# Key normalisation through a logarithm and an exponential on ScalarE, and two small TensorE products moved later, in a two-block hybrid model on one core

## The chip, the core and the metric

One Trainium2 chip, one of its cores. The metric is the device time of one execution in microseconds (us); lower is better. TensorE runs the products, VectorE (DVE in the rows), ScalarE (ACT) and GpSimd (POOL) run the elementwise work, SyncE (SP) issues the loads.

## The reference, cut to what matters

The kernel computes two transformer blocks, one after the other, for 512 tokens of width 1024: a gated-delta-rule block and then a block with stick-breaking attention and an RWKV-7 time mix, each with its feed-forward layers, all in f32. The change lies in the second block, between the projection by `w_in` and the scans. There every channel group of the RWKV part needs its key normalised per head, its decays and its bonus:

```python
p = p + (p_prev - p) * mu
w = -jax.nn.softplus(-(w0 + jnp.tanh(xw) @ w_up)) - 0.5
decay = jnp.exp(-jnp.exp(w.astype(jnp.float32)))
a = jax.nn.sigmoid(a0 + xa @ a_up)
kk = (k * k_k).astype(jnp.float32).reshape(B, L, H, N)
kk = kk / jnp.maximum(jnp.sqrt(jnp.sum(kk * kk, axis=-1, keepdims=True)), 1e-12)
k = k * (1.0 + (a - 1.0) * k_a)
...
bonus = jnp.sum(rh * kh * r_k.astype(jnp.float32), axis=-1, keepdims=True) * vh
```

## The kernel before

Every large product takes f32 operands as two parts, upper and lower (`HH`, `HL` for the activations, `WH`, `WL` for the weights), and sums three products of parts. A slab is 128x1024 numbers of weights (512 KB). SyncE loads it into one of four buffers `RAWS`; ScalarE copies its upper part into one of three buffers `WH` (line 1622, called through `begin`, always two slabs ahead); GpSimd subtracts it to get `WL` (line 2090); TensorE runs it in eight blocks of six matmuls (line 489, `slab_gemm`).

The stage of the change projects four groups, i = 0 to 3, of 128 channels. A group has six slabs. Three are of the RWKV part, for r, k and v, which VectorE takes out of PSUM and mixes with the token before (`shifted`, lines 1392, 1394, 1396, into `R1`, `K1`, `VB`). Three are of the attention, for q, k and v (`attention_inputs`, lines 1411 and 1413, 1417, 1422), after which TensorE transposes the attention's v (line 846) and ScalarE copies the transposes out (lines 1958, 1960).

Beside the three attention slabs run the `features` of the group. TensorE: the low-rank products (line 820), the sum of squares of the key over a head (line 826, into banks 4 and 5 of PSUM), the bonus product (line 834, bank 6). VectorE: `cs` (1431), `kk` (1433), `dcs` (1436), `max` (1438), `rec` (1440), `kn` (1443), `f1` (1446), `wc` (1447), `f2` (1451), `bm` (1453), `f3` (1457), `tm` (1459), `kf` (1461), `f4` (1464), `bo` (1466), `bn` (1473). ScalarE: two sigmoids (1926, 1931), `sq` (1936), the square root (1939), two exponentials (1942, 1944) and a third (1947).

Each engine's queue is written by generators: `alternate(features(i), ai, ai, ai)` takes one step of `features` and then three steps of `attention_inputs`, in turn, on each engine by itself. On TensorE a step of the latter is one block of a slab, so a `yield` more in `features` puts what follows it three blocks later. Nothing but semaphores ties the engines together, and each executes its queue in order: an instruction that waits holds all behind it. The waits that matter:

- line 826 waits for `sq` on ScalarE, and this for `kk` on VectorE;
- line 834 waits for `bo` on VectorE, the end of the chain of features;
- line 846 waits for the attention's v in SBUF (line 1422), which stands behind the features in VectorE's queue;
- the first slab product of a bank pair waits until VectorE has emptied it two slabs earlier (`shifted_bank`);
- after the last group, the heads and the scan of the next stage (from line 938 and line 865 on) wait for a memset on GpSimd (line 2195), and this for `bn` of group 3.

`EX` is one scratch tile. It holds the squares, then the clamped sums, the root, its reciprocal, and then the exponentials, so these steps follow one another. Two functions of ScalarE that are not in one table need a load of the other table between them.

Of the kernel before, what the change touches and what calls it, by code (L numbers as in the profile page):

```python
# [100 lines left out]
def alternate(*streams):  # L101

    live = list(streams)
    while live:
        for s in list(live):
            if next(s, alternate) is alternate:
                live.remove(s)


def finish(stream):  # L110
    for _ in stream:
        pass
# [34 lines left out]
def program(nc, xT, metaT, cols, consts, slabs, lup, gup, out):  # L147
    f32, f32r = mybir.dt.float32, mybir.dt.float32r
    ALU, ACT = mybir.AluOpType, mybir.ActivationFunctionType
# [6 lines left out]
    def steps(name, *names):  # L156
        return Steps(sem(name), *names)
# [205 lines left out]
    sh = steps("sh", "diff", "mix")  # L363
    lx = steps("lx", "tanh", "copy", "sigm")
    fp = steps("fp", "w", "a", "sq", "bon")
    fa = steps("fa", "sw", "sa", "sq", "rt", "e1", "e1p", "e2")
    fd = steps("fd", "cs", "kk", "dcs", "max", "rec", "kn", "f1", "wc", "f2", "bm", "f3", "tm", "kf", "f4", "bo", "bn")
    at_ev = steps("at_ev", "q0", "q1", "k", "v")
    at_vt = steps("at_vt", "t0", "t1")
    at_tr = count("at_tr")  # L370
# [106 lines left out]
    def tensor():  # L477
# [328 lines left out]
        def projected(which, j, job, ready=None):  # L806
            return slab_gemm(which, j, shifted_bank(job), HH, HL, KT, H2, ready)
# [4 lines left out]
        def features(i):  # L812
            te.wait_ge(s_k2, 64)
            if i:
                te.wait_ge(*fd.at("max", i - 1))
                te.wait_ge(*fd.at("bn", i - 1))
            te.wait_ge(*lx.at("copy"))
            for nm, r0, pr_ in (("w", 0, 2), ("a", 32, 3)):
                for q in range(2):
                    ins = te.matmul(pair(pr_)[:, q, :], LUP[r0:r0 + 32, 128 * i:128 * i + 128],  # L820
                                    LX[r0:r0 + 32, 264 * q:264 * q + 264], start=True, stop=True)
                ins.then_inc(*fp.up(nm, i))
            yield
            te.wait_ge(*fa.at("sq", i))
            for q in range(2):
                ins = te.matmul(PS[:, 4 + q, 0:288], con("bones"), EX[:, 288 * q:288 * q + 288], start=True, stop=True)
            ins.then_inc(*fp.up("sq", i))
            yield
            yield
            yield  # L830
            yield
            yield
            te.wait_ge(*fd.at("bo", i))
            te.matmul(bank(6), con("bones"), K1[:, 64:TP], start=True, stop=True).then_inc(*fp.up("bon", i))
            yield

        def attention_inputs(i):
            for s in range(3):
                yield from projected("w_in2", 12 + 4 * s + i, 2 + 7 * i + 3 + s)
            yield  # L840
            te.wait_ge(*at_ev.at("v", i))
            ps = shifted_bank(2 + 7 * i + 6)
            b = 2 * ((2 + 7 * i + 6) % 2)
            for j in range(5):
                o = PS[:, b, 128 * j:128 * j + 128] if j < 4 else PS[:, b + 1, 0:128]
                ins = te.transpose(o, VS[:, 128 * j:128 * j + 128], con("ident"))
            ins.then_inc(*at_tr.up(i))

        for i in range(4):
            for s in range(3):  # L850
                finish(projected("w_in2", 3 * i + s, 2 + 7 * i + s))
            ai = attention_inputs(i)
            alternate(features(i), ai, ai, ai)


        def rw_prepare(n):
# [155 lines left out]
    def vector():  # L1012
# [411 lines left out]
        def features(i):  # L1424
            yield
            ve.wait_ge(*fa.at("sw", i))
            ve.wait_ge(s_k2, 64)
            if i:
                ve.wait_ge(*fa.at("e2", i - 1))
                ve.wait_ge(*fd.at("f3", i - 1))  # L1430
            ve.tensor_tensor_scan(CS, RES[:, :], SW, 0.0, ALU.mult, ALU.add).then_inc(*fd.up("cs", i))
            ve.wait_ge(*sh.at("mix", 2 + 3 * i + 1))
            ve.tensor_scalar(KK, K1, col("kk", i), None, ALU.mult).then_inc(*fd.up("kk", i))
            yield
            ve.wait_ge(*fd.at("cs", i))
            ve.tensor_tensor(SW, CS, SW, ALU.subtract).then_inc(*fd.up("dcs", i))
            ve.wait_ge(*fp.at("sq", i))
            ve.tensor_scalar(two(EX), PS[:, 4:6, 0:288], 1e-24, None, ALU.max).then_inc(*fd.up("max", i))
            ve.wait_ge(*fa.at("rt", i))
            ve.reciprocal(EX, EX).then_inc(*fd.up("rec", i))  # L1440
            yield
            ve.wait_ge(*fd.at("rec", i))
            ve.tensor_tensor(KK, KK, EX, ALU.mult).then_inc(*fd.up("kn", i))
            ve.wait_ge(*fa.at("e1", i))
            ve.wait_ge(*sh.at("mix", 2 + 3 * i))
            ve.tensor_tensor(AR[:, i, :, 1, :], ch(R1), ch(EX), ALU.mult).then_inc(*fd.up("f1", i))
            ve.tensor_copy(WCC[:, i, :], ch(EX)[:, :, 63]).then_inc(*fd.up("wc", i))
            yield
            ve.wait_ge(*fa.at("e1p", i))
            ve.wait_ge(*fd.at("kn", i))  # L1450
            ve.scalar_tensor_tensor(AR[:, i, :, 0, :], ch(KK), -1.0, ch(SW), ALU.mult, ALU.mult).then_inc(*fd.up("f2", i))
            ve.wait_ge(*fd.at("f2", i))
            ve.tensor_tensor(KK, KK, SA, ALU.mult).then_inc(*fd.up("bm", i))
            yield
            ve.wait_ge(*fd.at("bm", i))
            ve.wait_ge(*fa.at("e2", i))
            ve.tensor_tensor(BK[:, i, :, 0, :], ch(KK), ch(EX), ALU.mult).then_inc(*fd.up("f3", i))
            ve.wait_ge(*f_kam.at(0))
            ve.tensor_scalar(SA, SA, col("ka", i), KAM[:, i:i + 1], ALU.mult, ALU.add).then_inc(*fd.up("tm", i))
            ve.wait_ge(*fd.at("tm", i))  # L1460
            ve.tensor_tensor(K1, K1, SA, ALU.mult).then_inc(*fd.up("kf", i))
            yield
            ve.wait_ge(*fd.at("kf", i))
            ve.tensor_tensor(BK[:, i, :, 1, :], ch(K1), ch(EX), ALU.mult).then_inc(*fd.up("f4", i))
            ve.wait_ge(*fd.at("f4", i))
            ve.scalar_tensor_tensor(K1[:, 64:TP], R1[:, 64:TP], col("rk", i), K1[:, 64:TP], ALU.mult,
                                    ALU.mult).then_inc(*fd.up("bo", i))
            yield
            ve.wait_ge(*fp.at("bon", i))
            ve.wait_ge(*sh.at("mix", 2 + 3 * i + 2))  # L1470
            if i == 3:
                ve.wait_ge(s_bs[0], 16)
            ve.tensor_tensor(TMP[i % 3][:, 0:512], VB[:, i, 128:64 + TP], bank(6), ALU.mult).then_inc(*fd.up("bn", i))

        for i in range(4):
            if i:
                ve.wait_ge(*fd.at("bn", i - 1))
            else:
                ve.wait_ge(*lx.at("sigm"))
            for s, dst in enumerate((R1, K1, VB[:, i, 64:64 + TP])):  # L1480
                shifted("w_in2", 3 * i + s, 2 + 3 * i + s, 2 + 7 * i + s, dst, 4 * s + i, 128)
            ai = attention_inputs(i)
            alternate(features(i), ai, ai, ai)


        def rw_prepare(n):
# [124 lines left out]
    def scalar():  # L1611
# [309 lines left out]
        def features(i):  # L1921
            ae.wait_ge(*fp.at("w", i))
            ae.wait_ge(*fz.at("sw"))
            if i:
                ae.wait_ge(*fd.at("f2", i - 1))
            ae.activation(two(SW[:, PAD:TP]), pair(2), ACT.Sigmoid, bias=col("w0", i)).then_inc(*fa.up("sw", i))
            ae.wait_ge(*fp.at("a", i))
            ae.wait_ge(*fz.at("sa"))
            if i:
                ae.wait_ge(*fd.at("kf", i - 1))  # L1930
            ae.activation(two(SA[:, PAD:TP]), pair(3), ACT.Sigmoid, bias=col("a0", i)).then_inc(*fa.up("sa", i))
            yield
            ae.wait_ge(*fd.at("kk", i))
            if i:
                ae.wait_ge(*fd.at("f4", i - 1))
            ae.activation(EX, KK, ACT.Square).then_inc(*fa.up("sq", i))
            yield
            ae.wait_ge(*fd.at("max", i))
            ae.activation(EX, EX, ACT.Sqrt).then_inc(*fa.up("rt", i))
            yield  # L1940
            ae.wait_ge(*fd.at("kn", i))
            ae.activation(EX, CS, ACT.Exp, scale=-KAPPA).then_inc(*fa.up("e1", i))
            ae.wait_ge(*fd.at("dcs", i))
            ae.activation(SW, SW, ACT.Exp, scale=-KAPPA).then_inc(*fa.up("e1p", i))
            yield
            ae.wait_ge(*fd.at("wc", i))
            ae.activation(EX, CS, ACT.Exp, scale=KAPPA).then_inc(*fa.up("e2", i))
            yield
# [509 lines left out]
```

## Time and profile before

| what | value |
|---|---|
| three runs | 2178.99, 2170.0 and 2177.69 us, median 2177.69 |
| the profiled execution's own time | 2169.75 us |
| its span | 2168.5 us |
| mean granted clock of TensorE | 0.966 |
| busy | PE 92%, PE weight load 77%, DVE 37%, POOL 35%, ACT 33% |
| the stage of the four groups | about 1216 to 1418 us from the start |

The profiled execution lies 0.25 us below the fastest of the three runs and 7.94 us below their median. A busy share is one of the whole span; what the change does is decided in the stage, whose own rows stand further below.

### The profile page before, as it was taken

Reading aid. Unit: us, or ns where it says so; the run is one execution under the profiler, and the core shown is the slowest. Engines: PE = TensorE matmul, PEld = TensorE weight load, DVE = VectorE, ACT = ScalarE, POOL = GpSimd, SP = SyncE. Lnnn points to the kernel's source line nnn. Section 1 sums busy time; section 2 is a strip of 40 time slices with the busy share of each in tenths; the row PEclk is TensorE's granted clock in tenths of the full one; section 3 lists DMA queues with packets and bytes.
Section 4 is the critical chain, followed back from the end, with each engine's and each line's share of the span. In section 5 each row is a group of like instructions: output and inputs, shape, how many; then the busy total and the mean of one; then the engine's idle time right before and its main releaser. Section 6 shows DMA issues by size and latency. Waiting matters only on the chain. (4 is left out here: it accounts for less than half of the span.)

```text
span 2168.5 us, 32158 instructions
## 1 busy us (share of the span) xinstructions
PE 1991.5 (92%) x13960; PEld 1674.6 (77%) x13960; DVE 794.9 (37%) x1065; ACT 705.6 (33%) x1056; POOL 763.2 (35%) x444
## 2 busy tenths in 40 slices
PE   3889988999999999999999888888999789999997
PEld 2657767777888889999999877866666568888885
DVE  6664453232111013443310466643443433434201
ACT  2453221333222333222222333254554333222222
POOL 2322120434444554444444332211111144444453
PEclk9999999999999999999999999998998899999999
DMA  7332220324332232232222422100000322332331
GB/s 272 115 119 98 79 79 32 116 78 145 117 97 90 90 102 88 88 94 91 84 88 93 131 59 63 30 6 2 2 2 2 126 69 89 96 97 89 98 91 62
DMA packets 55723, 182.76 MB, mean 84 GB/s; under 512 B 7552, under 2 KB 7808, under 8 KB 55456
## 3 DMA queue, kind: packets, MB, share of 16 engines
q1 hardware_dynamic: 55584, 180.72, 25.4%
q8 instruction: 110, 1.80, 0.3%
q14 instruction: 29, 0.24, 0.0%
HBM read 175.45 MB, written 5.24 MB: 83 GB/s over the span
## 5 line engine op out<-in xcount | busy, mean ns | idle before, releaser
L2090 POOL TENSOR_TENSOR WL<-RAWS,WH 128x1024 fp32r<-128x1024 f32 (+2 forms) x275 | 649.0, 2363 | 983.4 <-ACT WH L1622 983.4
L489 PE MATMUL PS<-HH,WH 128*128 128x264 f32 (+2 forms) x2184 | 673.1, 350 | 48.4 <-issue 12.9
L489 PE MATMUL PS<-HL,WH 128*128 128x264 f32 (+2 forms) x2184 | 657.4, 343 | 0.0
L489 PE MATMUL PS<-HH,WL 128*128 128x264 f32 (+2 forms) x2184 | 654.3, 341 | 0.0
L489 PEld LDWEIGHTS PS<-HH,WH 128*128 128x128 f32 (+1 forms) x2184 | 380.7, 192 | 117.4 <-issue 36.6
L1622 ACT ACTIVATE WH<-RAWS 128x1024 fp32r<-128x1024 f32 (+2 forms) x275 | 283.9, 1033 | 455.1 <-PE PS L489 402.1
L489 PEld LDWEIGHTS PS<-HH,WL 128*128 128x128 f32 (+1 forms) x2184 | 380.5, 191 | 48.4 <-issue 0.4
L489 PEld LDWEIGHTS PS<-HL,WH 128*128 128x128 f32 (+1 forms) x2184 | 380.9, 191 | 47.1 <-issue 1.6
L489 PE MATMUL PS<-IHf,WH 128*128 128x512 f32 (+1 forms) x704 | 209.4, 338 | 0.0
L489 PE MATMUL PS<-IHf,WL 128*128 128x512 f32 (+1 forms) x704 | 209.2, 338 | 0.0
L489 PE MATMUL PS<-ILf,WH 128*128 128x512 f32 (+1 forms) x704 | 209.2, 338 | 0.0
L1369 DVE TENSOR_TENSOR TMP<-TMP,PS 128x512 f32<-128x512 f32 (+1 forms) x66 | 45.8, 693 | 251.0 <-PE PS L489 244.0
L1889 ACT ACTIVATE IHf<-TMP 128x512 fp32r<-128x512 f32 (+1 forms) x66 | 42.0, 636 | 283.2 <-DVE TMP L1369 283.2
L489 PEld LDWEIGHTS PS<-ILf,WH 128*128 128x128 f32 x704 | 120.6, 188 | 14.9
L489 PEld LDWEIGHTS PS<-IHf,WH 128*128 128x128 f32 x704 | 120.5, 188 | 14.8
L489 PEld LDWEIGHTS PS<-IHf,WL 128*128 128x128 f32 x704 | 120.4, 188 | 14.9
L1364 DVE TENSOR_TENSOR TMP<-TMP,RSTD 128x528 f32<-128x528 f32 (+1 forms) x44 | 104.5, 2375 | 41.1 <-ACT TMP L1885 41.1
L1376 DVE SCALAR_TENSOR_TENSOR X<-PS,X 128x528 f32<-128x528 f32 (+1 forms) x16 | 11.2, 700 | 222.5 <-PE PS L489 222.5
L1357 DVE TENSOR_TENSOR TMP<-PS,RSTD 128x528 f32<-128x528 f32 (+1 forms) x44 | 30.8, 700 | 150.9 <-PE PS L489 150.2
L2106 POOL TENSOR_TENSOR SQA<-SQA,TMP 128x512 f32<-128x512 f32 (+1 forms) x39 | 54.9, 1408 | 80.4 <-ACT TMP L1635 79.7
L1371 DVE TENSOR_TENSOR ILf<-TMP,IHf 128x512 fp32r<-128x512 f32 (+1 forms) x66 | 48.7, 737 | 46.4 <-ACT IHf L1889 46.4
L1635 ACT ACTIVATE TMP<-X 128x512 f32<-128x512 f32 (+1 forms) x42 | 26.1, 627 | 86.7 <-DVE X L1376 35.7
(493 smaller groups left out, 1917.0 us busy)
## 6 DMA issues: line engine op xcount, KB each, us to landing
RAWS<-w_w_in SPq DMA_DIRECT2D x52, 512.0 KB, 4.3
RAWS<-w_ada SPq DMA_DIRECT2D x32, 512.0 KB, 3.6
RAWS<-w_f0g SPq DMA_DIRECT2D x22, 512.0 KB, 3.6
RAWS<-w_f0u SPq DMA_DIRECT2D x22, 512.0 KB, 3.5
RAWS<-w_f1g SPq DMA_DIRECT2D x22, 512.0 KB, 3.6
RAWS<-w_f1u SPq DMA_DIRECT2D x22, 512.0 KB, 3.6
RAWS<-w_f2g SPq DMA_DIRECT2D x22, 512.0 KB, 3.5
RAWS<-w_f2u SPq DMA_DIRECT2D x22, 512.0 KB, 3.5
```

Of the source, the lines that this page charges most:

```text
L489: ins = te.matmul(ps[0:m, q, o:o + b - a] if len(halves) > 1 else ps[0:m, o:o + b - a], w[:, k * m:k * m + m], v[:, k0 + k, a:b], start=fi ...
L1357: ve.tensor_tensor(tv, place(f, 2 * j), r, ALU.mult).then_inc(*ff_g.up("g", FT * (f - 1) + j))
L1364: ve.tensor_tensor(tv, tv, r, ALU.mult).then_inc(*ff_g.up("r", FT * (f - 1) + j))
L1369: ve.tensor_tensor(tv, tv, place(f, 2 * j + 1), ALU.mult).then_inc(*ff_mul.up(FT * f + j))
L1371: ve.tensor_tensor(IL[f][:, j, :], t, IH[f][:, j, :].bitcast(f32), ALU.subtract).then_inc(*ff_lo.up(FT * f + j))
L1376: ve.scalar_tensor_tensor(xv, place(f, 2 * FT + m), 0.5 if f else MOD[:, 40 + m:41 + m], xv, ALU.mult, ALU.add).then_inc(*ff_x.up(8 * f + m))
L1622: ae.activation(WH[s % NS][:, 0:n], RAW[i % NR][:, 0:n], ACT.Copy).then_inc(*w_hi.up(s))
L1635: ae.activation((TMP[k % 3] if k else SQA)[:, 0:n], X[:, k, t0:T2], ACT.Square).then_inc(*n_sq.up(8 * SQUARED[q] + k))
L1889: ae.activation(IH[f][:, j, :], t, ACT.Copy).then_inc(*ff_hi.up(FT * f + j))
L2090: ge.tensor_tensor(WL[s % NS][:, 0:n], RAW[i % NR][:, 0:n], WH[s % NS][:, 0:n].bitcast(f32), ALU.subtract).then_inc(*w_lo.up(s))
L2106: ge.tensor_tensor(SQA[:, 0:n], SQA[:, 0:n], TMP[k % 3][:, 0:n], ALU.add).then_inc(*n_acc.up(added(q, k)[1] - 1))
```

## The change

Three edits, all in the features stage. The reciprocal on VectorE goes, and the square root on ScalarE becomes a logarithm and then an exponential with scale -0.5, both in one table that is loaded right behind `sq`. The sum of squares stands three blocks later in TensorE's queue. The bonus product and the VectorE step that multiplies it with v become functions of their own: on TensorE behind the first slab of the next group (for group 3 behind the transposes), on VectorE at the end of the group.

```diff
@@ steps
-    fa = steps("fa", "sw", "sa", "sq", "rt", "e1", "e1p", "e2")
-    fd = steps("fd", "cs", "kk", "dcs", "max", "rec", "kn", "f1", ...
+    fa = steps("fa", "sw", "sa", "sq", "ln", "rt", "e1", "e1p", "e2")
+    fd = steps("fd", "cs", "kk", "dcs", "max", "kn", "f1", ...
@@ tensor
             yield
+            yield
             te.wait_ge(*fa.at("sq", i))
             for q in range(2):
                 ins = te.matmul(PS[:, 4 + q, 0:288], con("bones"), EX[:, 288 * q:288 * q + 288], start=True, stop=True)
             ins.then_inc(*fp.up("sq", i))
-            yield
-            yield
-            yield
-            yield
-            yield
+
+        def bonus(i):
             te.wait_ge(*fd.at("bo", i))
             te.matmul(bank(6), con("bones"), K1[:, 64:TP], start=True, stop=True).then_inc(*fp.up("bon", i))
-            yield
@@
         for i in range(4):
             for s in range(3):
                 finish(projected("w_in2", 3 * i + s, 2 + 7 * i + s))
+                if i and s == 0:
+                    bonus(i - 1)
             ai = attention_inputs(i)
             alternate(features(i), ai, ai, ai)
+        bonus(3)
@@ vector
             ve.tensor_scalar(two(EX), PS[:, 4:6, 0:288], 1e-24, None, ALU.max).then_inc(*fd.up("max", i))
+            yield
             ve.wait_ge(*fa.at("rt", i))
-            ve.reciprocal(EX, EX).then_inc(*fd.up("rec", i))
-            yield
-            ve.wait_ge(*fd.at("rec", i))
             ve.tensor_tensor(KK, KK, EX, ALU.mult).then_inc(*fd.up("kn", i))
@@
-            yield
+
+        def bonus(i):
             ve.wait_ge(*fp.at("bon", i))
             ve.wait_ge(*sh.at("mix", 2 + 3 * i + 2))
@@
             alternate(features(i), ai, ai, ai)
+            bonus(i)
@@ scalar
             yield
+            log_and_exp()
             ae.wait_ge(*fd.at("max", i))
-            ae.activation(EX, EX, ACT.Sqrt).then_inc(*fa.up("rt", i))
+            ae.activation(EX, EX, ACT.Ln).then_inc(*fa.up("ln", i))
+            ae.wait_ge(*fa.at("ln", i))
+            ae.activation(EX, EX, ACT.Exp, scale=-0.5).then_inc(*fa.up("rt", i))
```

ScalarE's queue in group 0, from `sq` to the third exponential, before (1939 is the root, 1942 and 1944 are `e1` and `e1p`, 1947 is `e2`):

```order
L1936 ACTIVATE X<-X 128x576 [waits fd]
L1939 ACT_TABLE_LOAD
L1939 ACTIVATE X<-X 128x576 [waits fd]
L1622 ACTIVATE WH<-RAWS 128x1024 [waits gemm,s_raw1]
L1942 ACT_TABLE_LOAD
L1942 ACTIVATE X<-X 128x576 [waits fd]
L1944 ACTIVATE X<-X 128x576 [waits fd]
L1947 ACTIVATE X<-X 128x576 [waits fd]
```

The same place now (1940 is the logarithm, 1942 the exponential that ends the norm, 1945 and 1947 are `e1` and `e1p`, 1950 is `e2`):

```order
L1936 ACTIVATE X<-X 128x576 [waits fd]
L1629 ACT_TABLE_LOAD
L1940 ACTIVATE X<-X 128x576 [waits fd]
L1942 ACTIVATE X<-X 128x576 [waits fa]
L1622 ACTIVATE WH<-RAWS 128x1024 [waits gemm,s_raw1]
L1945 ACTIVATE X<-X 128x576 [waits fd]
L1947 ACTIVATE X<-X 128x576 [waits fd]
L1950 ACTIVATE X<-X 128x576 [waits fd]
```

One load of a table stands where two stood, and the weight copy has two activations and no load ahead of it.

VectorE's queue at the end of group 0, before (1464 and 1466 are `f4` and `bo`, 1473 is `bn`, 1422 the attention's v, 1392 the first step of the next group's r):

```order
L1464 TENSOR_TENSOR BK<-X 128x9x64 [waits fd]
L1466 SCALAR_TENSOR_TENSOR X<-X,CV 128x512 [waits fd]
L1473 TENSOR_TENSOR TMP<-VB,PS 128x512 [waits sh,fp]
L1422 TENSOR_TENSOR VS<-PS,RSTD 128x528 [waits fz,gemm]
L1392 TENSOR_TENSOR SG<-PS,RSTD 128x528 [waits sh,gemm,fd]
```

The same place now (`bo` is 1464, `bn` is 1472):

```order
L1462 TENSOR_TENSOR BK<-X 128x9x64 [waits fd]
L1464 SCALAR_TENSOR_TENSOR X<-X,CV 128x512 [waits fd]
L1422 TENSOR_TENSOR VS<-PS,RSTD 128x528 [waits fz,gemm]
L1472 TENSOR_TENSOR TMP<-VB,PS 128x512 [waits sh,fp]
L1392 TENSOR_TENSOR SG<-PS,RSTD 128x528 [waits sh,gemm,fd]
```

`bn` stands behind the attention's v and still ahead of the next group's r.

## Rows read from the trace of the kernel before

**Rows 1.** Windows: length, busy PE, PEld, DVE, ACT, POOL, granted clock, DMA, GB/s.

```profile
1235.00:1420.00 185.00, 152.87 (x1098) 142.77 (x1099) 116.39 (x110) 55.68 (x67) 47.35 (x21) 0.93 0.17 51
1425.00:1700.00 275.00, 249.52 (x3243) 185.79 (x3242) 117.41 (x261) 130.82 (x290) 37.07 (x90) 0.90 0.01 2
```

**Rows 2.** The waits, 1225 to 1425 us: us in total, times, longest.

```profile
PE PS L834 <- DVE X L1466: 14.3, 4, 4.7
PE PS L826 <- ACT X L1936: 13.7, 4, 3.4
PE PS L846 <- DVE VS L1422: 3.2, 4, 0.8
```

**Rows 3.** The timeline of TensorE: start, us, line, count, [idle before <- what ended it].

```profile
1235.01 1.17 PE L820 MATMUL PS<-LX,LUP 32*128 32x264 f32 x8
...
1241.96 1.24 PE L826 MATMUL PS<-X,KC 128*128 128x288 f32 x4 [3.42 <-ACT X L1936]
1242.82 0.63 PE L489 MATMUL PS<-HH,WH 128*128 128x264 f32 x2
1243.28 0.40 PE L489 MATMUL PS<-HL,WH 128*128 128x264 f32 x2
...
1263.18 0.64 PE L489 MATMUL PS<-HH,WH 128*128 128x264 f32 x2
...
1266.78 0.77 PE L846 MATMUL PS<-KC,VS 128*128 128x128 f32 x5 [0.80 <-DVE VS L1422]
1267.30 0.49 PE L489 MATMUL PS<-HH,WH 128*128 128x264 f32 x2
...
1285.01 1.17 PE L820 MATMUL PS<-LX,LUP 32*128 32x264 f32 x8
...
1336.41 1.17 PE L820 MATMUL PS<-LX,LUP 32*128 32x264 f32 x8
...
1343.36 2.29 PE L826 MATMUL PS<-X,KC 128*128 128x288 f32 x4 [3.41 <-ACT X L1936]
...
1387.93 1.17 PE L820 MATMUL PS<-LX,LUP 32*128 32x264 f32 x8
...
1419.20 0.34 PE L938 MATMUL PS<-QA,KA 64*128 64x128 f32 x1 [0.95 <-ACT VT L1960]
```

**Rows 4.** The timeline of VectorE, group 0, and one row of group 3.

```profile
1243.23 0.76 DVE L1438 TENSOR_SCALAR X<-PS 128x576 f32<-128x576 f32 x1 [1.38 <-PE PS L826]
1244.74 3.75 DVE L1440 RECIPROCAL X<-X 128x576 f32<-128x576 f32 x1 [0.75 <-ACT X L1939]
...
1249.02 2.08 DVE L1443 TENSOR_TENSOR X<-X 128x576 f32<-128x576 f32 x1
1251.85 0.76 DVE L1446 TENSOR_TENSOR AR<-X 128x576 f32<-128x576 f32 x1 [0.75 <-ACT X L1942]
...
1254.68 2.74 DVE L1457 TENSOR_TENSOR BK<-X 128x576 f32<-128x576 f32 x1
...
1259.53 0.75 DVE L1466 SCALAR_TENSOR_TENSOR X<-X,CV 128x512 f32<-128x512 f32 x1
1262.10 0.69 DVE L1473 TENSOR_TENSOR TMP<-VB,PS 128x512 f32<-128x512 f32 x1 [1.81 <-PE PS L834]
...
1403.16 0.75 DVE L1443 TENSOR_TENSOR X<-X 128x576 f32<-128x576 f32 x1
```

**Rows 5.** The timeline of ScalarE, group 0.

```profile
1241.92 1.28 ACT L1939 ACT_TABLE_LOAD   x1
1244.03 0.69 ACT L1939 ACTIVATE X<-X 128x576 f32<-128x576 f32 x1 [0.82 <-DVE X L1438]
1246.95 1.06 ACT L1622 ACTIVATE WH<-RAWS 128x1024 fp32r<-128x1024 f32 x1 [2.24 <-PE PS L489]
```

**Rows 6.** The timeline of GpSimd: a weight subtraction in group 0, and the next stage's first memset.

```profile
1248.09 2.40 POOL L2090 TENSOR_TENSOR WL<-RAWS,WH 128x1024 fp32r<-128x1024 f32 x1 [7.21 <-ACT WH L1622]
...
1418.37 0.52 POOL L2195 MEMSET V<- 64x512 f32 x1 [24.57 <-PE PS L846]
```

More of the change, by code:

```diff
@@ L365, in program @@
     fp = steps("fp", "w", "a", "sq", "bon")
-    fa = steps("fa", "sw", "sa", "sq", "rt", "e1", "e1p", "e2")
-    fd = steps("fd", "cs", "kk", "dcs", "max", "rec", "kn", "f1", "wc", "f2", "bm", "f3", "tm", "kf", "f4", "bo", "bn")
+    fa = steps("fa", "sw", "sa", "sq", "ln", "rt", "e1", "e1p", "e2")
+    fd = steps("fd", "cs", "kk", "dcs", "max", "kn", "f1", "wc", "f2", "bm", "f3", "tm", "kf", "f4", "bo", "bn")
     at_ev = steps("at_ev", "q0", "q1", "k", "v")
```

## The prediction

> **What bounds the kernel now.** I read the page first (TensorE busy for 92% of the span, no other engine over 37%), so only what makes TensorE idle or slow can count. Then the windows of the stage and of the one behind it [rows 1]: in 185 us of the four groups TensorE works 152.9, and its granted clock is 0.93 where steady slabs have 1. Then the waits of the stage [rows 2]: three kinds of wait make up nearly all of it, 14.3 us for the bonus product, 13.7 us for the sum of squares, 3.2 us for the transposes, 31.2 us together. None is for weights, so neither loads nor the weight split bound the stage. The timelines of the engines then give the lengths [rows 3 to 6]. I write times within a group from the start of its low-rank product (1235.01 us in group 0).
>
> The groups follow one another at 1235.01, 1285.01, 1336.41 and 1387.93 us, and the next stage begins at 1419.20 [rows 3]: lengths of 50.0, 51.4, 51.5 and 31.3 us (the last without the next group's three slabs). A block of a slab takes (1285.01 - 1267.30) / 24 = 0.74 us, a slab 5.9 [rows 3].
>
> **The sum of squares, three blocks later.** It starts when the squares are ready, at 1241.96, or 6.95; TensorE then has been idle for 3.42 us, since 3.53 [rows 3]. What makes the squares late (the v mix, `cs`, `kk`) is not touched, so 6.95 stays. Three blocks ahead of it fill 2.2 of the 3.42 us: 1.2 us stay. The product itself is unchanged and the next block follows 0.86 us behind it, at 7.8 [rows 3]. Two blocks are left of the attention's q slab then, not five, so it ends at 9.3, and the k and v slabs end at 15.2 and 21.1 if nothing else holds them.
>
> **The reciprocal.** Before, `max` starts at 8.2 and ends at 9.0, the root runs from 9.0 to 9.7, the reciprocal from 9.7 to 13.5 (3.75 us), and after the two steps on the attention's q `kn` starts at 14.0 [rows 4, 5]. Now: the logarithm starts at 9.0 like the root (0.69 us) and the exponential behind it takes as long, to 10.4. No row shows either function on this tile; between the bounds of nothing and 1.4 us more, I take the root's 0.69 [rows 5], the same engine and shape. VectorE does the q steps at 9.4 to 10.15 meanwhile, as the slab ends at 9.3, so `kn` starts at 10.45 instead of 14.0: 3.55 us earlier. The reciprocal's 3.75 us leave VectorE, and the exponential's 0.69 are on ScalarE, where it is idle.
>
> **The tables.** The load ran right behind the squares, 1241.92 to 1243.20, and the root started at 1244.03 when `max` was done [rows 4, 5]. The new load stands at the same place and is hidden by the same wait, and the second load goes, which was hidden too. The edit is worth nothing; were the cover gone it would cost at most 1.28 us a group. The Trainium skill (ScalarE: Activation LUTs, What ACT_TABLE_LOAD costs) adds a drain of 1.38 us to the load's 1.28. By that rule the root could not have started before 1244.56; the trace does not agree. By it the logarithm would start 0.54 us later, some 1.6 us over the groups whose chain decides.
>
> **What is late next: the weight split.** Behind the exponential stands the weight copy, free to run from 9.3 (end of the q slab), so it runs 10.45 to 11.5 and GpSimd's subtraction 11.6 to 14.0 (1.06 and 2.40 us) [rows 5, 6]. A VectorE step with its operands in SBUF that starts while GpSimd works there is held: `kn` at 1249.02 took 2.08 us and ended at 1251.10, 0.61 us after GpSimd at 1250.49; unheld it takes 0.75 [rows 4, 6]. The rule for this is in the Trainium skill (SBUF — State Buffer, SBUF: two separate sides: the pair of ports that VectorE and GpSimd share is a lock, and the loser waits for the whole instruction); by it the trace agrees, and without it the sum would be about 5 us larger. Now `kn` escapes (10.45 to 11.2), `e1` runs 11.55 to 12.25, and `f1`, which would start at 12.3, is held to 14.6. `f1` to the start of `f3` was 1252.61 to 1254.68, so `f3` starts at 16.7. The second split of the group (free at 15.2, behind `e2`) meets `f3` again as before (2.74 us), so the rest to the end of `bo` is 5.6 us as before: 1254.68 to 1260.28 [rows 4]. `bo` ends at 22.3, before at 25.3: 3.0 us earlier.
>
> **The bonus product.** Its wait of 4.7 us disappears: it now stands a slab behind the transposes, some 6 us, when `bo` is long done. Its 0.86 us (by the like product of line 826 at full clock) move into the stretch between the transposes and the next group. What is late next is the transposes: the attention's v leaves PSUM behind `bo`, at 22.35, and the transposes follow 0.76 us later, at 23.1, while the v slab ended at 21.1. So their wait grows from 0.8 to 2.0 us. On VectorE `bn` now waits for the bonus product, with the next group's r mix queued behind it. That starts about 1.27 + 0.69 = 2.0 us later than the end of its slab; its three steps take 4.3 to 5 us, the k slab ends 6.8 us later, and its banks are wanted only then: nothing on the path. SyncE's store of `bn` of groups 0 to 2 moves too; its queue has already issued all but one weight load by then, and the later ones wait for nothing that TensorE needs: nothing.
>
> **The end of group 3.** No split runs here (`kn` 0.75 us [rows 4]), `bo` ends at about 19.5, and the v slab at 21.1 decides: transposes at 21.95. Behind them come 0.5 us of transposes, the bonus product (1.27 us to its reader), `bn` (0.69) and GpSimd's memset (0.52) [rows 3, 4, 6]: the next stage starts at 25.1, where before it was 31.3. The new chain behind the transposes costs about 1.5 us more than the old one and is counted in this.
>
> **Sum.** From one group's start to the next: 23.1 + (1285.01 - 1266.78) + 0.86 = 42.2 us [rows 3]. Gains: 50.0 - 42.2 = 7.8, 51.4 - 42.2 = 9.2, 51.5 - 42.2 = 9.3, 31.3 - 25.1 = 6.2: 32.5 us. This takes full clock for all. Some 18 us of it are idle time and 14 us are the low clock behind the long waits: a pair of slab matmuls at 1263.18 took 0.64 us, one at 1243.28 0.40 [rows 3]. In these rows the clock is full behind the wait of 0.80 us (1267.30: 0.49 us), and of the waits of 3.4 to 4.7 us it is low behind two of three (line 826 at 1343.36, the slab at 1263.18) [rows 3]; the new ones of 1.2 and 2.0 us are nearer to the first, and I take off 1.5 us. The gain is **31 us**: 2169.75 becomes 2138.8. The profiled execution was 7.9 us below the median of the three runs, so against that median I expect **2146.7 us**, a gain of 1.4%. A measurement of this kernel can tell about 0.5% (11 us) from no change.
>
> **Rivals.**
> *The low clock stays* (chance 0.17). If the waits of 1.2 and 2.0 us bring TensorE to 1.2 GHz as the long ones did, only the idle time comes back: 18 us, 2160. For it: behind a wait of 3.41 us in group 2 the product of line 826 took 2.29 us, behind one of 3.42 us in group 0 1.24 us [rows 3], so length alone does not decide.
> *The table's drain* (0.03). If the logarithm waits as the skill's rule would have it, 1.6 us less gain: 2148. Against it stands the root's start.
> *The chain of features keeps it* (0.08). If `f2`, `bm`, `kf`, `f4` are held by GpSimd also, each held step costs up to 2 us (2.74 against 0.75) and the wait for the transposes takes them all. With five of them in each of three groups, or three and the low clock kept, 30 or 18 + 14 us are given back, and the time is within 0.5% of before, about 2174. Against it: only two splits fall into the chain, and each holds VectorE once. The same time would come out if the change did not do what it says (separate tables for the two functions, two loads on the path): the order of the queue shows one load.
> *Slower* (0.03). Behind this stage comes a long one of small products and waits, 275 us with a mean clock of 0.90 [rows 1], so some 20% of it at half clock. It begins at another moment and after another pattern of waits. If the clock stayed low for much more of it, a pair of matmuls takes 0.24 us more (0.64 against 0.40) in a slot of 0.25 us (a third of a block), nearly 1 us per us of work. It outweighs 31 us from some 32 us of such work; low clock would then fill 55 + 64 of 307 us, a mean of 0.81. At a mean of 0.75 the stage would take 330 us, 55 more, and the time would be about 2202. Nothing in the rows asks for it.
>
> **Range.** The forecast's own case (0.69): at best the split misses `f1`, which gives 1.3 us in three groups, and the clock never falls, 2141; the three runs themselves spread over 9 us, so 2135 at the low end. The upper end takes in the kept clock: 2163. Faster by over 0.5%: 0.69 + 0.17 + 0.03 = 0.89; within it 0.08; slower 0.03.
>
> **What would show it.** In the profile after: waits for the sum of squares of 1.2 us each, for the bonus product none, for the transposes about 2 us in groups 0 to 2 and 0.9 in group 3; `kn` 10.4 us behind the group's start; `f1` held to 2 us; group lengths of 42.2 us and 25.1 us for the last; a clock of about 0.99 in the stage. Wrong would be: a wait of 3 us or more for the transposes, the logarithm starting over 0.1 us behind `max`, TensorE waiting for `WL`, or the stage behind it longer than before by more than 3 us.

## The result, and the profile after

| | runs | median | lowest to highest |
|---|---|---|---|
| before | 4 | 2176.26 us | 2170.0 to 2178.99 |
| changed | 4 | 2139.89 us | 2135.34 to 2145.26 |

The changed kernel takes 0.984 of the time of before, 95% interval 0.982 to 0.986: 1.6% faster. I had forecast 2146.7 us, in a range of 2135 to 2163, and a gain of 31 us; the medians are 36.4 us apart. The profiled execution of the changed kernel took 2141.41 us, its span 2140.2.

TensorE in the timeline of the changed kernel, where [rows 3] stood before. Lines have moved: 827 is the sum of squares, 843 the transposes, 832 the bonus product.

```profile
1240.14 1.17 PE L820 MATMUL PS<-LX,LUP 32*128 32x264 f32 x8
...
1247.14 1.24 PE L827 MATMUL PS<-X,KC 128*128 128x288 f32 x4 [1.27 <-ACT X L1936]
...
1263.09 0.77 PE L843 MATMUL PS<-KC,VS 128*128 128x128 f32 x5 [1.56 <-DVE VS L1422]
...
1269.55 1.02 PE L832 MATMUL PS<-X,KC 128*128 128x512 f32 x2
...
1282.19 1.17 PE L820 MATMUL PS<-LX,LUP 32*128 32x264 f32 x8
...
1324.25 1.17 PE L820 MATMUL PS<-LX,LUP 32*128 32x264 f32 x8
...
1366.30 1.17 PE L820 MATMUL PS<-LX,LUP 32*128 32x264 f32 x8
...
1388.47 0.77 PE L843 MATMUL PS<-KC,VS 128*128 128x128 f32 x5 [0.80 <-DVE VS L1422]
1389.08 1.02 PE L832 MATMUL PS<-X,KC 128*128 128x512 f32 x2
1391.46 0.37 PE L938 MATMUL PS<-QA,KA 64*128 64x128 f32 x1 [1.36 <-POOL V L2198]
```

The groups now follow one another after 42.05, 42.06 and 42.05 us, and the last takes 25.16. The bonus product waits for nothing. The four groups take 151.3 us where they took 184.2. The waits of TensorE, against [rows 2] (us in total, times, longest):

```profile
PE PS L843 <- DVE VS L1422: 5.5, 4, 1.6
PE PS L827 <- ACT X L1936: 5.1, 4, 1.3
```

The window of the stage shows a granted clock of 1.00 where [rows 1] had 0.93 (columns: length, busy PE, PEld, DVE, ACT, POOL, clock, DMA, GB/s):

```profile
1240.00:1391.00 151.00, 139.52 (x1086) 132.61 (x1084) 101.44 (x106) 52.85 (x67) 47.42 (x20) 1.00 0.20 61
```

VectorE and ScalarE in group 0, against [rows 4, 5]. The root's place is held by the logarithm (1940) and the exponential (1942), the reciprocal is gone; 1433 is `kk`, 1441 `kn`, 1444 `f1`, 1457 `tm`, 1464 `bo`:

```profile
1243.79 2.59 DVE L1433 TENSOR_SCALAR X<-X,CV 128x576 f32<-128x576 f32 x1
...
1248.42 0.76 DVE L1438 TENSOR_SCALAR X<-PS 128x576 f32<-128x576 f32 x1 [1.38 <-PE PS L827]
...
1250.64 0.76 DVE L1441 TENSOR_TENSOR X<-X 128x576 f32<-128x576 f32 x1
1252.17 2.48 DVE L1444 TENSOR_TENSOR AR<-X 128x576 f32<-128x576 f32 x1 [0.76 <-ACT X L1945]
...
1257.39 2.65 DVE L1457 TENSOR_SCALAR X<-X,CV,KAM 128x576 f32<-128x576 f32 x1
...
1261.66 0.75 DVE L1464 SCALAR_TENSOR_TENSOR X<-X,CV 128x512 f32<-128x512 f32 x1
```

```profile
1247.11 1.28 ACT L1629 ACT_TABLE_LOAD   x1
1249.21 0.69 ACT L1940 ACTIVATE X<-X 128x576 f32<-128x576 f32 x1 [0.82 <-DVE X L1438]
1249.93 0.69 ACT L1942 ACTIVATE X<-X 128x576 f32<-128x576 f32 x1
```

GpSimd subtracts weights three times in the same stretch, and `kk`, `f1` and `tm` are the steps that each of these holds:

```profile
1243.65 2.40 POOL L2093 TENSOR_TENSOR WL<-RAWS,WH 128x1024 fp32r<-128x1024 f32 x1 [5.48 <-ACT WH L1622]
...
1251.64 2.39 POOL L2093 TENSOR_TENSOR WL<-RAWS,WH 128x1024 fp32r<-128x1024 f32 x1 [5.59 <-ACT WH L1622]
...
1256.92 2.80 POOL L2093 TENSOR_TENSOR WL<-RAWS,WH 128x1024 fp32r<-128x1024 f32 x1 [2.89 <-ACT WH L1622]
```

One wait is new and I had not seen it coming. It is in the waits at the start of the next stage (us in total, times, longest):

```profile
DVE X L1497 <- DMA bsave<-TMP: 2.7, 1, 2.7
```

VectorE begins the next stage by waiting 2.7 us for the stores of the bonus, and ScalarE waits 2.1 us for them.

To see what is the change's and what is not, I cut each profile in four: up to the first group, the four groups, the next stage (to the last copy of the attention's output, on ScalarE), and the rest. Before: 1235.0, 184.2, 273.1, 476.2 us. Changed: 1240.1, 151.3, 272.4, 476.3 us. The spans differ by 28.3 us because the first part, whose code is the same, was 5.1 us longer in this profile; over the fourteen profiles here it lies between 1235.0 and 1243.4. The stage's 32.9 us are the change's.

### The profile page after: what moved, and what is told of

It reads as the page before. It is cut to its first block and busy times, and to the rows that moved or that the text cites. A ratio compares the mean times of both kernels' runs of the same rounds, so it can differ in the third digit from the quotient of the medians.

```text
span 2140.2 us, 32154 instructions
## 1 busy us (share of the span) xinstructions
PE 1985.7 (93%) x13960; PEld 1672.0 (78%) x13960; DVE 780.6 (36%) x1061; ACT 702.8 (33%) x1056; POOL 763.3 (36%) x444
## 3 DMA queue, kind: packets, MB, share of 16 engines
q1 hardware_dynamic: 55584, 180.72, 25.7%
## 5 line engine op out<-in xcount | busy, mean ns | idle before, releaser
L489 PE MATMUL PS<-HH,WH 128*128 128x264 f32 (+2 forms) x2184 | 669.3, 348 | 48.8 <-issue 11.5
L489 PEld LDWEIGHTS PS<-HL,WH 128*128 128x128 f32 (+1 forms) x2184 | 379.3, 190 | 47.8 <-issue 1.9
L1371 DVE TENSOR_TENSOR ILf<-TMP,IHf 128x512 fp32r<-128x512 f32 (+1 forms) x66 | 49.1, 744 | 46.4 <-ACT IHf L1889 46.4
```

The lines of the kernel that those rows point to most:

```text
L489: ins = te.matmul(ps[0:m, q, o:o + b - a] if len(halves) > 1 else ps[0:m, o:o + b - a], w[:, k * m:k * m + m], v[:, k0 + k, a:b], start=fi ...
L1371: ve.tensor_tensor(IL[f][:, j, :], t, IH[f][:, j, :].bitcast(f32), ALU.subtract).then_inc(*ff_lo.up(FT * f + j))
```

## The experiments

The stage's length is read from one profile each, first low-rank product to the next stage's first product. Where two profiles of the same program were taken it came out as 148.29 and 148.24 us, or 139.06 and 139.08, far steadier than the whole. In both of these programs TensorE keeps the full clock through the four groups. Where it does not, the first three groups of one profile differ by up to 2.7 us (44.9 and 47.6 below), and the table has one profile for each version, so a difference of one or two microseconds between such rows says little. Each row of the table is before with the edits that it names; each ratio is one of total times, against runs of before made beside it.

| | four groups | groups 0 / 1 / 2 / 3 | ratio to before, 95% |
|---|---|---|---|
| before | 184.2 | 50.0 / 51.4 / 51.5 / 31.3 | |
| logarithm only | 184.5 | 51.0 / 51.1 / 51.2 / 31.2 | 0.999 (0.998 to 1.000) |
| squares later only | 179.5 | 49.6 / 48.8 / 49.9 / 31.3 | 0.998 (0.997 to 0.999) |
| squares and bonus three blocks later | 166.6 | 44.9 / 47.6 / 47.6 / 26.4 | 0.993 (0.992 to 0.995) |
| bonus moved only | 170.7 | 46.4 / 47.8 / 47.8 / 28.7 | 0.992 (0.990 to 0.994) |
| logarithm and bonus | 167.1 | 46.3 / 45.4 / 46.5 / 28.9 | 0.991 (0.989 to 0.993) |
| squares and bonus | 162.9 | 45.3 / 45.4 / 46.5 / 25.7 | 0.991 (0.989 to 0.993) |
| the change | 151.3 | 42.1 / 42.1 / 42.1 / 25.2 | 0.984 (0.982 to 0.986) |

### The logarithm alone

```diff
-            ve.reciprocal(EX, EX).then_inc(*fd.up("rec", i))
...
-            ae.activation(EX, EX, ACT.Sqrt).then_inc(*fa.up("rt", i))
+            ae.activation(EX, EX, ACT.Ln).then_inc(*fa.up("ln", i))
+            ae.wait_ge(*fa.at("ln", i))
+            ae.activation(EX, EX, ACT.Exp, scale=-0.5).then_inc(*fa.up("rt", i))
```

> Only the logarithm and exponential in place of root and reciprocal; both products where they were. Theory 1 (one chain of features per group sets the end, through two waits of TensorE): the reciprocal's gain is mostly lost, since kn must then wait for the attention's q slab, which ends at 11.5 us of the group: bo ends some 1.5 us earlier, the wait for the bonus product falls from 4.7 to about 3.2 us in groups 0 to 2, the wait for the sum of squares stays 3.4. Four groups to the next stage: about 177 us instead of 184.2, the total 5 to 9 us less. Theory 2 (each edit takes away its own stall, and they add): the chain gets shorter by the whole 3.05 us of the reciprocal less the exponential in all four groups, 12 us in all.

The four groups took 184.5 us, 0.3 more than before, and the time is 0.999 of before, barely clear of the noise. Theory 1 had `kn` waiting for the attention's q slab, but it left 1.5 us of gain in groups 0 to 2, and there was none. VectorE's timeline of group 1 (start of the group 1292.32) shows why:

```profile
1301.60 0.76 DVE L1438 TENSOR_SCALAR X<-PS 128x576 f32<-128x576 f32 x1 [2.43 <-PE PS L826]
1306.77 0.42 DVE L1411 SCALAR_TENSOR_TENSOR QA<-PS,RSTD 128x248 f32<-128x248 f32 x1 [4.42 <-PE PS L489]
...
1307.45 0.75 DVE L1441 TENSOR_TENSOR X<-X 128x576 f32<-128x576 f32 x1
```

VectorE stands idle for 4.42 us on the attention's q slab, in place of the reciprocal's 3.75 us. That slab ends late since TensorE waited 3.41 us for the squares and ran the blocks behind it at the low clock. So `kn` starts 15.1 us into the group; in group 1 before it started at 15.1 as well (1300.07, with the group at 1285.01). `kn` is no longer held by GpSimd (0.75 us, before 2.42), but `f1` is in its place (2.12 us, before 0.76). So the bonus product starts 26.7 us into the group, as before. TensorE waits less for it (11.8 us in all against 14.3 of [rows 2]) only because the slower clock brings it there later.

### The squares later, with and without the bonus product

The second edit is one `yield` more. I first tried it like this, which moves the bonus product by three blocks too, since it stands behind it in the same generator; my expectation overlooks that:

```diff
             yield
+            yield
             te.wait_ge(*fa.at("sq", i))
```

> Only the sum of squares three blocks later. Theory 1: its wait falls from 3.4 to 1.2 us, but the chain behind it does not get shorter, so the same 2.2 us come back as a longer wait for the bonus product (about 6.9 us): the four groups take 184 us less what the clock gives, 181 to 184, total within 3 us of before. Theory 2 (the edits add): 2.2 us in each of four groups, 9 us less.

The groups took 166.6 us, 17.6 less, where I had expected 181 to 184. Then I took away one `yield` behind the product, so that only the squares' product moves:

```diff
             yield
+            yield
             te.wait_ge(*fa.at("sq", i))
...
             ins.then_inc(*fp.up("sq", i))
             yield
             yield
             yield
             yield
-            yield
```

> Reciprocal kept, sum of squares three blocks later, bonus product in its old place (in the run with the sum of squares alone it had moved three blocks along with it). Theory 1: bo ends at 24.05 us of the group as there, the bonus product waits about 5.6 us instead of 3.45 and four blocks and the slow clock follow, group length about 48.5 us, the four groups about 175 us. So of the 17.6 us of that run about half were the bonus product's move. Theory 2 (the earlier sum of squares did it all by the clock): about 167 us again.

179.5 us, and the total 0.998 of before. The waits of TensorE over the stage, in the run with both later and then in the one with the squares alone:

```profile
PE PS L835 <- DVE X L1467: 11.8, 4, 3.5
PE PS L827 <- ACT X L1937: 5.1, 4, 1.3
PE PS L847 <- DVE VS L1423: 3.2, 4, 0.8
```

```profile
PE PS L834 <- DVE X L1466: 20.3, 4, 5.6
PE PS L827 <- ACT X L1936: 5.1, 4, 1.3
PE PS L846 <- DVE VS L1422: 3.2, 4, 0.8
```

The wait for the squares falls from 13.7 to 5.1 us in both. With the bonus product in its place, 6.0 us come back as a longer wait for it: theory 1's account, though I had expected 175 us. The longest wait is the 5.6 us that I had expected, so it is the low clock behind it that I had put at too little. Moved three blocks along, the product waits less than before (11.8 against 14.3), so 12.9 of the 17.6 us of the first run were the bonus product's move.

### The bonus product alone, and the change less one edit

The third edit alone is that of the diff above, on TensorE and on VectorE.

> Only the bonus product behind the next group's first slab, reciprocal kept. Theory 1: no wait for it, but the attention's v leaves PSUM only behind bo at 25.3 us of the group, so the transposes wait about 2.8 us instead of 0.8; group length about 45.2 us, the four groups about 164 us, total some 20 us less. Theory 2: the wait of 4.7 us and its low clock go and nothing comes in their place, group length about 43.5 us. A third possibility, that the moved product and the step bn before the next group's r mix cost something: then the wait of the k projection's consumer would show it, and VectorE's idle before line 1392 of the k slab would be gone.

170.7 us against 164 expected: the wait for the transposes was 2.46 us, as theory 1 has it (2.8), and the third possibility did not come: VectorE still waits 1.65 us for the k slab before it mixes it. Group 0 took 46.4 us and the others 47.8, above the 45.2 of the sum. What the sum lacks is the low clock, in two places. In groups 1 to 3 the product of the squares takes 2.29 us behind its wait, in group 0 1.24, and this is the 1.4 us between the groups. The other place is behind the wait for the transposes, in groups 0 to 2:

```profile
1265.24 1.33 PE L842 MATMUL PS<-KC,VS 128*128 128x128 f32 x5 [2.46 <-DVE VS L1421]
1266.22 0.79 PE L489 MATMUL PS<-HH,WH 128*128 128x264 f32 x2
1266.80 0.64 PE L489 MATMUL PS<-HL,WH 128*128 128x264 f32 x2
```

A pair of matmuls takes 0.64 us, the low clock, where the changed kernel had 0.41 behind its wait of 1.56. The kernel with the first and the third edit:

> The change without its second edit: logarithm and exponential, bonus moved, sum of squares where it was. Theory 1: the wait for the sum of squares is 3.4 us again, bo ends at about 23.8 us, the v slab at 23.3, the transposes wait about 1.3 us; group length about 43.7 us instead of 42.05, the four groups about 158 us instead of 151.3. So the second edit is worth some 7 us here, and nothing alone. Theory 2: it is worth 9 us in both.

It took 167.1 us, not 158. The wait for the transposes is 1.20 us, theory 1's 1.3, and that for the squares 3.41. Behind the latter the product takes 2.29 us, against 1.24 in the change, and the pairs that follow 0.64:

```profile
1296.63 2.29 PE L826 MATMUL PS<-X,KC 128*128 128x288 f32 x4 [3.41 <-ACT X L1935]
1298.30 1.05 PE L489 MATMUL PS<-HH,WH 128*128 128x264 f32 x2
1299.15 0.64 PE L489 MATMUL PS<-HL,WH 128*128 128x264 f32 x2
```

So the second edit, worth 4.7 us alone, is worth 15.8 us with the other two. Last, the kernel without the first edit:

> The change without its first edit: root and reciprocal kept, both moves made. Theory 1: bo ends at 24.05 us of the group, the attention's v leaves PSUM behind it, the transposes start at 24.8 us where the v slab ended at 21.1, a wait of 3.6 us, with a fall of the clock likely behind it; group length 43.9 to 45.4 us, the four groups 159 to 163 us. So the first edit, worth nothing alone, is worth 8 to 12 us with the other two. Theory 2 (edits add, and the first is worth nothing): 151 us as with the whole change.

162.9 us, within what was expected: the wait for the transposes is 3.3 us in groups 0 to 2, and the first edit is worth 11.6 us here and nothing alone. The edits do not add: alone they give 0, 4.7 and 13.5 us, 18 together, and the change gives 32.9. The ratios of the totals say the same: 3, 5 and 17 us alone, 25 together, and 35 for the change. A version with the first two edits and without the third was not run.

### The table's load without its cover

```diff
-            log_and_exp()
             ae.wait_ge(*fd.at("max", i))
+            log_and_exp()
             ae.activation(EX, EX, ACT.Ln).then_inc(*fa.up("ln", i))
```

> The whole change with the load of the table placed behind the wait for max, so that nothing hides it. Theory 1 (the load costs its 1.28 us and was hidden): the logarithm starts 1.28 us later, kn and bo with it, the transposes wait 2.8 us instead of 1.56 in groups 0 to 2, group length about 43.3 us; in group 3 the v slab decides and nothing changes; the four groups about 155 us instead of 151.4. Theory 2 (a drain goes with each load, 2.66 us in all): the logarithm starts 2.66 us behind max, and the four groups take about 159 us.

ScalarE in group 0:

```profile
1247.85 1.28 ACT L1629 ACT_TABLE_LOAD   x1 [2.11 <-DVE X L1438]
1249.14 0.69 ACT L1940 ACTIVATE X<-X 128x576 f32<-128x576 f32 x1
```

The logarithm starts 1.29 us behind the load's start: that is theory 1. The drain of 1.38 us that the Trainium skill adds (ScalarE: Activation LUTs, What ACT_TABLE_LOAD costs) is not in this trace. ScalarE had been idle ahead of this load, which leaves open that a drain comes only behind an activation. The trace of before has such a load at the end of the stage, between two activations, and it shows none either:

```profile
1418.78 0.27 ACT L1960 ACTIVATE VT<-PS 128x128 f32<-128x128 f32 x1
1419.07 1.28 ACT L1629 ACT_TABLE_LOAD   x1
1420.36 0.28 ACT L2003 ACTIVATE TMP<-PS 128x128 f32<-128x128 f32 x1
```

The transposes wait 2.80 us, as expected. But the groups took 44.8 us, not 43.3, and all four 159.5 (the total is 0.989 of before, 0.986 to 0.993): the number of theory 2, by another way. Behind the wait of 2.80 us the clock falls (0.97 over the stage, 1.00 in the change), a few pairs of matmuls later:

```profile
1262.96 0.76 PE L843 MATMUL PS<-KC,VS 128*128 128x128 f32 x5 [2.80 <-DVE VS L1422]
...
1264.67 0.65 PE L489 MATMUL PS<-HL,WH 128*128 128x264 f32 x2
```

The cover is worth 8 us. The longer waits are 3.7 us of it (1.24 in each of three groups), and the clock is the rest.

### What the change leaves

Two waits stay, and VectorE is held by GpSimd before each: `kk` (2.59 us) ahead of the squares, `f1` and `tm` ahead of the transposes. First, the bonus product where TensorE waits anyway, behind the v slab and ahead of the transposes:

```diff
             yield
+            bonus(i)
             te.wait_ge(*at_ev.at("v", i))
...
-                if i and s == 0:
-                    bonus(i - 1)
...
-        bonus(3)
```

> The change with the bonus product not behind the next group's first slab but between the v slab and the transposes, where TensorE waits anyway. Theory 1: groups 0 to 2 get 0.6 us shorter (41.4 us), and the last ends 1.2 us earlier, with the wait of the next stage's first VectorE step for the store of the bonus gone: the four groups about 148 us instead of 151.3, the next stage 1 to 2 us shorter than with the change. Theory 2 (the place of the product does not matter): 151.3 us.

148.3 us, groups of 41.5 us, as theory 1 has them. The next stage took 265.3 us, but not because the wait for the store had gone: it was still 2.7 us, and VectorE's first step came 1.7 us behind the stage's start in place of 2.0. I come back to it below. Second, one split later, on top of the change alone:

```diff
             for s in range(3):
-                begin("w_in2", 12 + 4 * s + i, 2, last)
-                for _ in range(7):
+                for t in range(7):
+                    if t == (0 if s else 3):
+                        begin("w_in2", 12 + 4 * s + i, 2, last)
                     yield
```

> The whole change, and only the first weight split of each group moved behind the squares. Theory 1: kk is no longer held, the squares and their sum come 2 us earlier and TensorE does not wait for them, but the logarithm, kn and all behind still meet the second and third split: the wait for the transposes stays, at about 1.5 to 2 us since the slabs end 1.3 us earlier too. Group length 41 us, the four groups 146 to 148 us. Theory 2: only both moves together help, 151 us.

145.2 us, a little under theory 1's 146 to 148: TensorE no longer waits for the squares, and 1.56 us for the transposes stay. The total was 0.983 of before (0.980 to 0.986). Third, with the bonus product in the gap and the third split of a group behind the copy of the transposes as well (the condition is `if s < 2 and t == (0 if s else 3)`):

> As the run before, and the weight splits moved in ScalarE's queue: the first of a group behind the squares, the third behind the copy of the transposes. Theory 1 (VectorE's steps kk and tm are held only because GpSimd subtracts then, and this sets both waits that are left): kk takes 0.6 us instead of 2.6, the sum of squares waits no more, tm takes 0.6 us, bo ends at about 19 us, the transposes wait 0.8 us with the bonus product in that gap; group length about 39.0 us, the four groups about 140 us, total 10 to 12 us below the change. Theory 2: the later splits make TensorE wait for WL, which the waits would show, and the time is the change's or worse.

139.1 us, groups of 38.9 us against 39.0 expected. VectorE in group 0, `kk` at 1431 and `tm` at 1455, held no more:

```profile
1245.39 0.50 DVE L1431 TENSOR_SCALAR X<-X,CV 128x576 f32<-128x576 f32 x1
...
1252.23 2.49 DVE L1442 TENSOR_TENSOR AR<-X 128x576 f32<-128x576 f32 x1 [0.77 <-ACT X L1943]
...
1257.47 0.57 DVE L1455 TENSOR_SCALAR X<-X,CV,KAM 128x576 f32<-128x576 f32 x1
```

`f1` (1442) is still held, and no longer matters: no matmul in TensorE's timeline of the four groups waits any more. The second split could be moved too; nothing waits for what it would give.

Yet the totals did not follow at first: 2133.2 us with the bonus product in the gap and 2131.8 with the splits moved, 1.4 us for 9.2. Their next stages took 265.3 and 274.3 us. Both were run again side by side:

> The version with the bonus product in the gap again, since its four groups took 9.2 us longer than with the splits moved but its next stage, whose code is the same, 9 us less at a clock of 0.95 instead of 0.91. Theory 1 (the clock of the next stage varies from run to run and with where it begins): the four groups again 148.3 us, the next stage anywhere from 265 to 274 us, and over more runs this version is some 5 us or more slower than the one with the splits moved. Theory 2 (ending the stage this way keeps the clock): 265 us again, and both versions the same.

> The version with the splits moved again, beside the run before. Theory 1: the four groups 139.1 us, the next stage 265 to 274 us, total some 5 us or more below the run before. Theory 2: next stage 274 us again, total the same as the run before.

The stages came out at 148.2 and 139.1 us again, but the next stage of the first at 272.2. The window of that stage, in the first and in the second run of the version with the product in the gap:

```profile
1386.00:1652.00 266.00, 241.27 (x3239) 179.34 (x3241) 118.00 (x263) 132.91 (x296) 35.93 (x90) 0.95 0.01 3
```

```profile
1389.00:1661.00 272.00, 249.13 (x3234) 185.69 (x3234) 117.64 (x262) 132.13 (x294) 35.19 (x88) 0.91 0.01 2
```

A clock of 0.95 in one execution and 0.91 in the next, with the same program. Over the repeated runs the medians were 2139.4 us (4 runs) and 2128.5 us (5 runs), 10.9 us apart. Against before, the version with the product in the gap came out at 0.980 (0.978 to 0.983) and then at 0.984 (0.982 to 0.986), and the one with the splits moved at 0.980 (0.978 to 0.982) and 0.979 (0.977 to 0.982); the change is at 0.984. By the length of the stage the version with the splits moved is the fastest, twice by 9.2 us; of the totals only the second comparison shows it. The next stage took 272.2 to 274.8 us in thirteen of the fourteen profiles, and the 265.3 stands alone: why that execution kept more of its clock is not known.

## Why the prediction was right, point by point

- **What bounds the kernel.** Right. The waits of TensorE in the stage were the place: with them down from 31.2 to 10.6 us, the stage went from 184.2 to 151.3.
- **The squares three blocks later.** Forecast 1.2 us of wait left, measured 1.27.
- **The reciprocal.** The logarithm started 9.07 us into the group (9.0) and took 0.69 us, as did the exponential; `kn` started at 10.50 (10.45). The root's duration, which I took between two bounds, was the value. There was luck in it: VectorE's two steps on the attention's q, which stand ahead of `kn`, ended at 10.49 and not at 10.15, just as the exponential did.
- **The tables.** One load, hidden; right behind the squares. I had said that the lost cover would cost at most 1.28 us a group. It cost 2.7, 1.24 of them as a longer wait and 1.5 by the clock, which I had not counted.
- **The weight split.** `kn` escaped (0.76 us), `f1` was held (2.48 us). The second to be held was `tm` and not `f3`, since `f3` started 0.19 us ahead of the subtraction, with the same sum: `bo` ended at 22.27 us (22.3).
- **The bonus product.** No wait. The transposes started at 22.95 (23.1) after 1.56 us of wait, not 2.0: the v slab ended at 21.4, not 21.1. The blocks were not slower (0.73 us each), but the pair behind the sum of squares took 0.2 us more than the others, and the slab's last pair ends 0.2 us behind the point where the next would start.
- **The group.** 42.05 us, forecast 42.2. Group 3: 25.16 us, forecast 25.1.
- **The clock.** I took off 1.5 us for a fall behind the new waits. None came. I had split the stage's gain into 18 us of idle time and 14 us of low clock; the waits fell by 20.6 us, so some 12 us are left for the clock.
- **SyncE's store.** This step failed, without a cost that can be seen. I priced the stores of groups 0 to 2 at nothing and left that of group 3 out. For it VectorE waits 2.7 us and ScalarE 2.1 at the start of the next stage, since `bn` of group 3 now ends 0.6 us before the stage begins. VectorE's first step there came 2.0 us behind the stage's start, before 1.5; the stage took 272.4 us, before 273.1.
- **The rivals.** The low clock did not stay: behind the waits of 1.27 and 1.56 us no pair is slow. That it was the right rival to fear, the experiments show: every version that left waits of 2.4 us or more had it. The table's drain is refuted by the run without cover and by the load at the end of the stage before. The chain of features was held twice behind `kn`, once by each split, as I had it against that rival. For a longer next stage nothing was seen.

The sum for the stage was 32.5 us, and 32.9 were measured. The medians differ by 36.4; the other 3.5 us are within the runs' own scatter (9 us before, 10 us after) and no row gives them a place. That the forecast lies 6.8 us above the median measured is these 3.5 us, the 1.5 us for the clock and 0.4 us of the sum, and 1.4 us by which the median of before fell with its fourth run.

## What to carry to other kernels

Where one engine waits twice on the same chain of another, both waits must be shortened together: the part that is left takes up the gain of the other, and here three edits gave 0, 4.7 and 13.5 us alone and 32.9 together. Follow the chain from the wait back through every engine, with what stands ahead of each step in its queue, and price each edit by where the next wait then ends. When one such wait is gone, look at which elementwise steps are held by another engine's long ones: moving one weight split in its queue gave a further 6.1 us, moving two and putting the bonus product into a gap 12.3 us.

## What the runs showed of the hardware

- TensorE's granted clock fell to its lower level (1.2 GHz; a pair of slab matmuls at 0.64 us against 0.41, or the sum of squares at 2.29 against 1.24) behind 35 of the 38 waits of 2.4 to 5.6 us that the stage has in all versions together, and behind none of 1.2 to 1.6 us. A wait of 2.80 us in place of 1.56 cost 1.5 us a group in clock on top of its own 1.24. The three long waits that did not do it are those of 3.42 us in group 0 of before, of 3.42 us in group 0 with the bonus moved only, and of 3.45 us in group 0 with the squares and the bonus three blocks later.
- The same program had a next stage of 265 us in one execution and of 272 in another, at a clock of 0.95 and of 0.91, and the first part, whose code never changes, took between 1235 and 1243 us. A difference of 10 us in a total of 2130 can hang on this. The length of the stage that was changed, read from one profile, repeated to 0.1 us in the two programs that were profiled twice, both with the full clock in it.
- A VectorE step that met a weight subtraction of GpSimd (2.4 to 2.8 us) took 2.48 to 2.65 us and ended 0.3 to 0.6 us behind it. With the subtraction moved, `kk` took 0.50 us in place of 2.59, and `tm` 0.57 in place of 2.65.
- A reciprocal of 128x576 numbers takes 3.75 us on VectorE, and an activation of the same size 0.69 us on ScalarE, whichever of root, logarithm and exponential it is.
- Behind a table's load of 1.28 us the next activation starts at once, whether ScalarE was idle ahead of the load (the run without cover: load at 1247.85, logarithm at 1249.14) or came straight from another activation (before: load at 1419.07, activation at 1420.36).
